# Turning the attention heads of two groups on VectorE and through DRAM, with their roots on GpSimd

## What is computed

```
def dilated_attention(q, k, v, gq, gk):
    q = rms_norm_2(q, gq)          # per head, over its 64 columns
    k = rms_norm_2(k, gk)
    for gi, (window, dilation) in enumerate(ATTN_GROUPS):
        o, l = _dilated_group(q[:, :, sl], k[:, :, sl], v[:, :, sl], window, dilation)
...
    scores = jnp.einsum('bdhnqe,bdhnke->bdhnqk', qb, kw).astype(jnp.float32) * (e ** -0.5)
```

## Time and profile before

| | |
|---|---|
| median of 3 runs | 788.85 us (788.71 to 788.95) |
| profiled execution | 788.89 us, of which the span of the profile is 787.1 us |
| PE busy | 781.6 us, 99% |
| VectorE busy | 594.1 us, 75% |
| ScalarE busy | 469.5 us, 60% |
| GpSimd busy | 4.5 us |
| DMA | 143.5 MB, mean 182 GB/s |

### The profile page before, as it was taken

The page is one execution under the profiler, slowest core; times in us unless marked ns, Lnnn a source line. Parts: engine busy times, 40 slices in busy tenths (PEclk is TensorE's granted clock), DMA queues, the critical chain, the costliest instruction groups (busy, mean ns, idle before and its releaser), DMA issues.

```text
span 787.1 us, 12689 instructions
## 1 busy us (share of the span) xinstructions
PE 781.6 (99%) x4940; PEld 661.1 (84%) x4940; DVE 594.1 (75%) x977; ACT 469.5 (60%) x673; POOL 4.5 (1%) x16
## 2 busy tenths in 40 slices
PE   9999999999999999999999999999999999999998
PEld 7888889888888888888888878888888888888886
DVE  6996889988788789779999864677776666556654
ACT  6876556655656567887566655756644554434542
POOL 0000000000000000000000000100000000000000
PEclk9999999999999999999999999999999999999999
DMA  9873344665556563746545386333755565665551
GB/s 322 291 257 108 108 161 161 204 209 175 192 186 208 180 251 104 234 147 215 183 157 187 117 256 219 108 104 112 228 177 183 179 191 170 209 208 174 184 181 53
DMA packets 84655, 143.52 MB, mean 182 GB/s; under 512 B 3904, under 2 KB 44672, under 8 KB 84352
## 3 DMA queue, kind: packets, MB, share of 16 engines
q1 hardware_dynamic: 83888, 141.82, 54.7%
q10 hardware_dynamic: 720, 1.05, 0.4%
HBM read 141.29 MB, written 1.05 MB: 181 GB/s over the span
## 4 chain that ended last, share of the span: by engine, by line
PE 92%; DVE 5%; ACT 1%; issue 1%; DMA 1%; ACTq 0%; DVEq 0%
PE bank L539 19%; PE bank L540 19%; PE bank L541 19%; PE bank L628 15%; PE bank L633 8%; PE bank L401 3%; PE bank L1048 2%; DVE w_lo L1914 1%; PE bank L1050 1%; PE bank L612 1%; PE bank L1191 1%; PE bank L1220 1%; DMA arena<-in_x_turned 1%; DVE arena L2431 1%; DVE stats L2461 1%
## 5 line engine op out<-in xcount | busy, mean ns | idle before, releaser
L1914 DVE TENSOR_TENSOR w_lo<-raw,w_hi 128x1024 fp32r<-128x1024 f32 (+1 forms) x254 | 302.2, 1214 | 52.5 <-ACT w_hi L1362 51.4
L1362 ACT CAST w_hi<-raw 128x1024 fp32r<-128x1024 f32 (+1 forms) x254 | 260.0, 1047 | 119.4 <-PE bank L541 107.9
L539 PE MATMUL bank<-w_hi,h_both 128*128 128x512 f32 x352 | 140.2, 398 | 0.4 <-DVE w_lo L1914 0.4
L540 PE MATMUL bank<-w_lo,h_both 128*128 128x512 f32 x352 | 137.3, 390 | 0.0
L541 PE MATMUL bank<-w_hi,h_both 128*128 128x512 f32 x352 | 137.3, 390 | 0.0
L539 PE MATMUL bank<-w_hi,a_both 128*128 128x512 f32 (+1 forms) x318 | 124.6, 392 | 0.1
L540 PE MATMUL bank<-w_lo,a_both 128*128 128x512 f32 (+1 forms) x318 | 123.5, 388 | 0.0
L541 PE MATMUL bank<-w_hi,a_both 128*128 128x512 f32 (+1 forms) x318 | 123.4, 388 | 0.0
L628 PE MATMUL bank<-a_both,w_hi 128*128 128x512 f32 x512 | 121.5, 389 | 0.0
L628 PEld LDWEIGHTS bank<-a_both,w_hi 128*128 128x128 f32 x512 | 95.5, 188 | 19.4
L539 PEld LDWEIGHTS bank<-w_hi,h_both 128*128 128x128 f32 x352 | 66.2, 188 | 14.8 <-issue 1.8
(11 more groups left out here) (242 smaller groups left out, 882.7 us busy)
## 6 DMA issues: line engine op xcount, KB each, us to landing
raw<-in_w_in SPq DMA_DIRECT2D x45, 1024.0 KB, 5.2
raw<-in_w_up SPq DMA_DIRECT2D x22, 1024.0 KB, 5.1
raw<-in_w_ff_up SPq DMA_DIRECT2D x16, 1024.0 KB, 5.5
raw<-in_w_ff_down SPq DMA_DIRECT2D x16, 1024.0 KB, 5.0
raw<-in_w_down SPq DMA_DIRECT2D x11, 1024.0 KB, 4.9
raw<-in_w_out SPq DMA_DIRECT2D x8, 1024.0 KB, 5.2
raw<-in_w_gla_branch SPq DMA_DIRECT2D x4, 1024.0 KB, 5.0
raw<-in_w_attn_branch SPq DMA_DIRECT2D x2, 1024.0 KB, 5.1
```

The source lines that it names most:

```text
L539: nc.tensor.matmul(dst, l_hi, r_hi, start=start, stop=False)
L540: nc.tensor.matmul(dst, l_hi, r_lo, start=False, stop=False)
L1362: nc.scalar.copy(dst, raw_half(m % RAW, half, size, cols)).then_inc(s.hi_done, 1)
L1914: nc.vector.tensor_tensor(dst, raw_half(n // 2 % RAW, n % 2, size, cols), h, ALU.subtract).then_inc(s.lo_done, 1)
```

## The change

- Groups 0 and 1: `turn_heads` moves from TensorE to VectorE. Each part is turned by two transposes of 32x32 blocks from `a_tok` into `blocked`. SyncE writes `blocked` to a DRAM scratch tensor in four DMAs of 256 KB (32 partitions each), and reads it back in two DMAs of 512 KB (128 partitions) with the blocks in their places. Keys are used as they land; ScalarE multiplies the queries by the gain (`heads_gained`, after chunks 5 and 8). The key gain is folded into the query gain.
- Group 2 stays on TensorE, in the middle of chunk 9, as before.
- Roots: VectorE only makes the guess, once for queries and keys together (32 columns); GpSimd makes the Newton steps. `over_rms` scales both parts in the turn of the values.
- VectorE takes one level in each turn of the loop in place of two in every second one; the last two are taken in turn 8.
- `att_score` reads keys of groups 0 and 1 in runs of 32 columns.

```diff
-LEVEL_VISITS = {1: ((LEVELS + 1, 6), (0, 4)), 3: ((2, 6), (1, 4)), 5: ((4, 6), (3, 4)), 7: ((6, 6), (5, 4)), 8: ((7, 4),)}
-TAKEN_BEFORE = {t: sum(len(v) for at, v in LEVEL_VISITS.items() if at < t) for t in range(12)}
+LEVEL_VISITS = {1: ((LEVELS + 1, 6), (0, 4)), 3: ((2, 6), (1, 4)), 5: ((4, 6), (3, 4)), 7: ((6, 6), (5, 4)), 8: ((7, 6),)}
+TAKEN_BEFORE = {1: 0, 3: 2, 5: 4, 7: 6, 8: 7}
...
+            def move_heads(g, i):
+
+                if i == 0:
+                    sp.wait_ge(s.heads_turned, 2 * g + 2)
+                if i < 2:
+                    for n in (2 * i, 2 * i + 1):
+                        sp.dma_start(crossing[g, :, :, n].rearrange("j c part t -> c j (part t)"),
+                                     blocked[g][32 * n:32 * n + 32].rearrange("p j part t -> p j (part t)")).then_inc(s.heads_out, 16)
+                if i == 2:
+                    sp.wait_ge(s.heads_out, 64 * (g + 1))
+                    if g >= 1:
+                        sp.wait_ge(s.att_T, g)
+                    for part in range(2):
+                        sp.dma_start(landed[g][:, part], crossing[g, :, :, :, part].rearrange("j c i t -> (j c) i t")).then_inc(s.heads_in, 16)
...
             for m in range(M_IN2 + 5, M_R + 2):
                 load(m)
+                for g in range(2):
+                    if 19 <= m - M_IN2 - 6 * g < 22:
+                        move_heads(g, m - M_IN2 - 6 * g - 19)
...
+            for g in range(AG + 1):
+                v = st[:, 48:80] if g < AG else st[:, 16:24]
+                y, t = [newton[:, i, 0:v.shape[1]] for i in range(2)]
+                gp.wait_ge(s.root_guessed, g + 1)
+                for step in range(3):
...
-                if t >= 3 and t % 3 == 0:
-                    turn_heads(t // 3 - 1, t)
+                if t == 3 * AG:
+                    pe.wait_ge(s.att_scaled, 2 * AG)
+                    pe.wait_ge(s.gla_taken, len(TAKEN))
...
+                            elif g == 1:
+                                keys = akT[1][r:r + AD, 2 * b:2 * b + 2, a, k0 * 32:k0 * 32 + 32]
+                                dst = dst.rearrange("p (i t) -> p i t", t=32)
+                            else:
+                                keys = akT[0][r:r + AD, :, :, k0 * 32:k0 * 32 + 32].rearrange("p i o t -> p o i t")
+                                dst = dst.rearrange("p (o i t) -> p o i t", o=TT, t=32)
...
+            def heads_gained(g):
+
+                act.wait_ge(s.heads_in, 32 * (g + 1))
+                for a in range(TT):
+                    v = landed[g][:, 0, :, a * P:(a + 1) * P].rearrange("p i (k t) -> p i k t", k=4)
+                    dst = aqT[g][:, :, a * P:(a + 1) * P].rearrange("p k (i t) -> p i k t", t=32)
+                    ins = nc.scalar.activation(dst, v, ACT.Copy, scale=column("attn_q_norm_g_2"))
+                ins.then_inc(s.att_T, 1)
...
+                        if g >= 1 and part < 2:
+                            act.wait_ge(s.heads_turned, 2 * g - 1 + part)
...
+                dve.wait_ge(s.root_found, t // 3 + 1)
+                r = st[:, 48:80].rearrange("p (part a h o) -> p part a h o", part=2, a=2, o=1)
+                for part in range(2):
...
+            def turn_heads(g, parts):
+
+
+                for part in parts:
+                    dve.wait_ge(s.att_scaled, 2 * g + part + 1)
+                    if g == 1:
+                        dve.wait_ge(s.heads_out, 64)
+                    for a in range(TT):
+                        dst = blocked[g][:, :, part, a * P:(a + 1) * P].rearrange("p j (k t) -> p k j t", k=4)
+                        ins = nc.vector.transpose(dst, a_tok[:, part, a, :].rearrange("p (k j c) -> p k j c", k=4, j=4))
+                    ins.then_inc(s.heads_turned, 1)
...
-                if 1 <= t <= 3 * AG and (t - 1) % 3 < 2:
-                    over_rms(t - 1)
+                if t < 3 * AG and t % 3 == 2:
+                    over_rms(t)
+                if t in (3, 6):
+                    turn_heads(t // 3 - 1, (0,))
...
+                if t in (3, 6):
+                    turn_heads(t // 3 - 1, (1,))
+                for nth in (8, 9) if t == 8 else (t,) if 1 <= t < 8 else ():
...
-                    inverse_root(st[:, 48:64], st[:, 48:64])
+                    if part == 1:
+                        dve.wait_ge(s.att_ms, nth + 1)
+                        root_guess(st[:, 48:80], st[:, 48:80], newton[:, 0], newton[:, 1]).then_inc(
+                            s.root_guessed, 1)
```

More of the change, by code:

```diff
@@ L61 @@
 LEVELS = 7
-LEVEL_VISITS = {1: ((LEVELS + 1, 6), (0, 4)), 3: ((2, 6), (1, 4)), 5: ((4, 6), (3, 4)), 7: ((6, 6), (5, 4)), 8: ((7, 4),)}
-TAKEN_BEFORE = {t: sum(len(v) for at, v in LEVEL_VISITS.items() if at < t) for t in range(12)}
+LEVEL_VISITS = {1: ((LEVELS + 1, 6), (0, 4)), 3: ((2, 6), (1, 4)), 5: ((4, 6), (3, 4)), 7: ((6, 6), (5, 4)), 8: ((7, 6),)}
+TAKEN_BEFORE = {1: 0, 3: 2, 5: 4, 7: 6, 8: 7}
+TAKEN = [level for visit in LEVEL_VISITS.values() for level in visit]
+VISITED = {lv: n + 1 for n, (lv, _) in enumerate(TAKEN)}
 VEC = {}
@@ L360, in two_blocks_kernel @@
         a_tok = area(12576, 2, TT, 512)
-        aqT = area(14624, 4 * AG, TOKENS)
-        akT = area(17696, 4 * AG, TOKENS)
+        aqT = [area(at, 4, TOKENS) for at in (14624, 15648, 11552)]
+        akT = [area(at, 4, TT, 4 * 32) for at in (19744, 18720)]
+        akT_last = area(17696, 4, TOKENS)
+        landed = [area(at, 2, 4, TT * 4 * 32) for at in (18720, 17696)]
+        blocked = [area(at, 4, 2, TT * 4 * 32) for at in (16672, 15648)]
+        crossing = nc.dram_tensor("heads_crossing", (AG - 1, 4, 32, 4, 2, TT * P), F32, kind="Internal").ap()
         av = area(20768, 3, TT, 512)
@@ L520, in link @@
                 gp.wait_ge(s.pool_chain, steps)
[L523 to L532, removed]
+            for g in range(AG + 1):
[3 more added lines that the diff above has]
+                for step in range(3):
+                    link(nc.gpsimd.tensor_tensor(t, y, y, ALU.mult))
+                    link(nc.gpsimd.tensor_tensor(t, t, v, ALU.mult))
+                    link(nc.gpsimd.tensor_scalar(t, t, -0.5, 1.5, ALU.mult, ALU.add))
+                    if step < 2:
+                        link(nc.gpsimd.tensor_tensor(y, y, t, ALU.mult))
+                nc.gpsimd.tensor_tensor(v, y, t, ALU.mult).then_inc(s.root_found, 1)
         @block.tensor
@@ L1080, in _ @@
             chunk_rows(n2 + 14, C_GLA + 4, 512, h)
[L1082 to L1095, removed]
             def level(t, first):
@@ L1184, in att_score @@
                 for g in range(AG):
[L1185 removed]
                     for b in range(2):
[L1187 to L1188 removed]
+                        tokens = a * P + 64 * b
+                        at = 0 if g == 0 else 2 * P + 64 * (b ^ (g - 1))
                         for e in range(2):
                             r = e * AD
[L1191 to L1192 removed]
+                            dst = bank[64 * b:64 * b + 64, 4 * e, at:at + (64 if g else TOKENS)]
+                            if g == 2:
+                                keys = akT_last[r:r + AD, k0, tokens:tokens + 64]
+                            elif g == 1:
[4 more added lines that the diff above has]
+                                dst = dst.rearrange("p (o i t) -> p o i t", o=TT, t=32)
+                            ins = nc.tensor.matmul(dst, aqT[g][r:r + AD, k0, tokens:tokens + 64], keys, start=True, stop=True)
                 ins.then_inc(s.att_scores, 1)
@@ L1714, in level_decay @@
                 nc.scalar.activation(z, z, ACT.Exp, scale=1.0 / 16).then_inc(s.gla_e, 1)
[L1716 to L1722, removed]
-                                         scale=column(("attn_q_norm_g_2", "attn_k_norm_g_2")[part])).then_inc(s.att_T, 1)
+            def heads_gained(g):
[5 more added lines that the diff above has]
+                ins.then_inc(s.att_T, 1)
             for t in range(3 * AG + 2):
@@ L1727, in _ @@
                 hi(n + 4, n + 5)
-                if t >= 3 and t % 3 == 0:
-                    heads_out(t // 3 - 1)
+                if t == 3 * AG:
+                    for part in range(2):
+                        act.wait_ge(s.att_turned, part + 1)
+                        dst, b = (aqT[2], akT_last)[part], 4 + 2 * part
+                        tiles = bank[:, b:b + 2, :].rearrange("p i (n t) -> p n i t", n=8)
+                        dst = dst.rearrange("p k (a i t) -> p (k a) i t", a=TT, i=2)
+                        if part == 0:
+                            nc.scalar.activation(dst, tiles, ACT.Copy, scale=column("attn_q_norm_g_2")).then_inc(s.att_T, 1)
+                        else:
+                            act.wait_ge(s.att_T, 2)
+                            nc.scalar.copy(dst, tiles).then_inc(s.att_T, 1)
                 hi(n + 6, n + 7)
@@ L1759, in _ @@
                     level_decay(t)
+                if t in (5, 8):
+                    heads_gained((5, 8).index(t))
             for a in range(TT):
@@ L1966, in rotate @@
```

(2 more changed lines are left out.)

67 lines of the change are left out of this document (33 added, 34 removed).

## The result

The changed kernel takes 791.92 us (median of 6 runs, 790.97 to 792.28), the kernel before 788.78 (6 runs, 788.67 to 789.06): a ratio of 1.0037, 95% interval 1.0027 to 1.0047. It is slower by 3.1 us, where 3.0 us of gain was forecast. The profiled execution of after has a span of 789.8 against 787.1, so 2.7 of the 3.1 are to be found in the two traces.

What follows compares the result with a forecast made beforehand. PE, busy 99% of the span, was taken as the bound. Transposes removed (2.70) and waits gone (0.86) give 3.56; 788.89 - 3.56 + 0.6 for VectorE's lateness = 785.9 us, range 785.1 to 788.3.

Steps and rivals of the forecast that it cites:

- Work taken from PE: Small transposes of groups 0 and 1 leave PE's queue, 1.35 us each: 2.70 gained.
- waits that go: PE's waits for VectorE at chunk 3 (0.30) and around the last level (0.15 and 0.41) vanish: 0.86 us.
- the sum of 3.56: Ideal gain in us: 2.70 from transposes taken off PE plus 0.86 from PE's waits that go.
- the 0.6 that was forecast: PE's lateness at group 2's turn, from longer GpSimd steps and semaphore delays in VectorE's chain: 0.6 us.
- VectorE's transposes: Eight transposes of 128x512, priced like elementwise passes at 0.60 us each, with ends of 0.3 and 1.2.
- GpSimd's steps: Newton steps: four pass under VectorE's work, eight take 2.3 us of its waiting; 32 columns add 0.03 a step.
- the walk: VectorE's queue followed from turn 4 to the last levels at 457.6, PE asking at 457.7: margin nil.
- The crossing: SyncE's DMA writes ahead of slabs 20 and 26: at 1.1 us a write, no slab lands late.
- Rival 3: Crossing writes from 32 partitions hold up slab 26: 791.7 us at 4.0 a write, otherwise 786.9 to 790; chance 0.12.
- rival 2: VectorE bounds turns 5 to 8 through slower transposes or GpSimd steps: 787.5 to 788.3 us; chance 0.22.
- gains: ScalarE's four query gains of 128x512, waiting for landed heads ahead of the rounding of chunks 7 and 10: no cost.
- scores: Score matmuls reading keys in runs of 32 columns: the pieces cost nothing.

Runs made afterwards that it cites:

- e7: The changed kernel with slabs 20 and 26 issued before the crossing writes, head roots back on VectorE and group 2 turned at the end of chunk 9: 785.33 us.
- e1: The changed kernel with SyncE issuing slab 20 (26) before its wait for turned heads, all four writes after it and the reads one slab later: 785.9 us.
- e2: The changed kernel with the head roots back on VectorE, in one piece of 32 columns once a group, crossing unchanged: 786.97 us.
- e10: The changed kernel with SyncE's wait for turned heads kept ahead of slabs 20 and 26, but the slab issued before the four writes: 786.25 us.
- e4: The changed kernel with 18 extra matmuls of 512 columns filling TensorE's wait before it turns group 2, results unread: 789.7 us.

## Why the prediction was wrong

**Work taken from PE, waits that go: right.** PE stood ready for group 2 at 457.75, forecast 457.7, and e7 reaches the sum of 3.56 in the time itself. The 0.44 that PE still waits in e1 answers to the 0.6 that was forecast.

**VectorE's transposes: nearly right.** Two at a time take 1.29, with a start 1.22 later of what follows, so 0.61 each against 0.60. Timeline of after:

```profile
390.40 1.29 DVE L2465 STREAM_TRANSPOSE arena<-arena 128x512 f32<-128x512 f32 x2
391.62 0.65 DVE L2439 TENSOR_TENSOR arena<-arena 128x512 f32<-128x512 f32 x1
```

**GpSimd's steps: mis-sized.** Timeline of GpSimd in after, the root of turn 5, beside the earlier trace rows:

```profile
411.96 0.58 POOL L552 TENSOR_TENSOR newton<-newton,stats 128x32 f32<-128x32 f32 x1
412.63 1.07 POOL L553 TENSOR_SCALAR newton<-newton 128x32 f32<-128x32 f32 x1
413.79 1.10 POOL L555 TENSOR_TENSOR newton<-newton 128x32 f32<-128x32 f32 x1
414.97 0.24 POOL L551 TENSOR_TENSOR newton<-newton 128x32 f32<-128x32 f32 x1
415.29 0.26 POOL L552 TENSOR_TENSOR newton<-newton,stats 128x32 f32<-128x32 f32 x1
```

As forecast, four steps pass under VectorE's two products and two remainders, each held for about the length of one of them, and eight follow. They come 0.32 apart (414.97 to the last start at 417.23, seven distances), where the steps of 8 columns of the kernel before come 0.29 apart (508.40 to 510.41, seven distances). So the allowance of 0.03 a step was right, and 0.24 a turn. But VectorE waits 2.74 and 2.75 instead of 2.3, 0.44 more. The missing 0.2 pass between the end of VectorE's remainders (414.78) and the first of the eight steps (414.97), and had no term. The larger fault was of place: the walk began with turn 4, so the wait in turn 2 cost nothing in it. But that wait holds the heads of group 0 that SyncE waits for, which in e2 left 0.96 sooner.

**The walk: right but for the crossing.** Its five marks were 410.3, 423.3, 435.3, 445.5 and 457.6. In e1 they come at 409.98, 423.50, 435.18, 445.19 and 457.94. In after the differences are +0.8, +1.35, +1.0, +3.65 and +4.24: slab 20 first, then GpSimd, then slab 26 with 2.6, then GpSimd again. The margin was called nil, and it was.

**The crossing: the step that failed.** The prediction said "with 1.1 a write nothing is late". It had slab 26 land at 438.9, 7.4 after the first write's issue at 431.5. It landed at 442.7, 9.7 after an issue at 432.98: 3.8 late in all. Of these, 1.5 is the later start, because VectorE was by then up to 1.35 behind its walk and SyncE waits for its heads. Only 0.3 is the write's size, 1.25 for each of two instead of 1.1. The other 2.0 had no term. They go with the two writes issued behind the slab, which the prediction left out of slab 26's sum: slab and writes were served together, 2.08 MB in the 8.4 us up to 442.2. An estimate from the rates of the two comes near that stretch: 5.0 for four writes at 1.25 and 2.6 for 1 MB at about 400 GB/s. How much of the 2.0 two writes behind would cost by themselves, no run shows (e10 has 0.8 for four behind a slab with a free start). Rival 3 named the right slab and the right path ("writes from 32 partitions hold up slab 26"), with a chance of 0.12. But by its own slope a write of 1.25 gives only 785.9 + 2 x 0.15 = 786.2. That its time of 791.7 for writes of 4.0 comes close to 791.92 is luck. The rival belonged much higher, as the term lay at a margin of zero and its price was in no row.

**The chances.** Two parts of the sum for "faster" don't fit the rivals' own ranges: rival 2, of 787.5 to 788.3, gives it two fifths, and rival 3, of 786.9 to 790 in its milder half, gives it 0.05 of 0.06.

**The clock: a missing term.** All waits were priced one for one. A wait of 4.24 cost 6.3, as PE works at the lower level for 4.7 us after it (461.99 to 466.7). Without it the time would be 791.92 - 2.06 = 789.9, near e4's: still above the high end of 788.3, but within 0.2% of before.

**GpSimd, gains, scores.** `heads_gained` held up no rounding that VectorE waited for, and both kernels' score matmuls take the same: 402 ns for one with 256 keys, before and after. Both had been costed at nothing. Groups of PE by line, of after, in the stretch of the scores (the row of before differs in the line number alone):

```profile
L1211 PE MATMUL bank<-arena 64*64 64x256 f32 x64 | 5.3, 402 | 0.0
```

## What to carry to other kernels

Where a step's margin comes out as zero, every unpriced term on its chain has to be put at its bad end, and the chain has to be followed through the queues of SyncE and DMA too: an engine that is late for a crossing is late again for whatever is loaded behind it. Issue loads with a date ahead of stores without one, in one queue, and spread a store over all 128 partitions. And price a wait of TensorE of several microseconds at more than its length: filling this one gave back a third of its cost.

## What the runs showed of the hardware

- Writes of 256 KB from 32 partitions ran at 198 to 219 GB/s, the same bytes from 128 partitions at 307 to 389, in rows of 2 KB both times.
- A 1 MB load lands 5.2 after its issue as a rule, 6.0 with four writes from 32 partitions issued behind it, 8.9 with two ahead and two behind, and 7.5 if these four are written from 128 partitions.
- After a wait of 4.24 us TensorE's granted clock was at its lower level for 4.7 us of work, at a cost of 2.06; after idle pieces of 0.7 and 0.9 it stayed full.
- VectorE's 32x32 transposes of 128x512 in f32 take 0.61 from start to start, as long as an elementwise pass.
- A GpSimd step, linked to the next by a semaphore, is 0.32 for 32 columns and 0.29 for 8.
